# First mixer of a block kernel: its first two column blocks as one, pooling products placed inside other blocks, decay and forget rows spread by transfers, step sizes multiplied into x

## The chip, the cores and the metric

The kernel runs on one core of a Trainium2 chip. The metric is the device time of one execution in microseconds, as the median of several. Engines are named as the profile does: PE is TensorE, DVE is VectorE, ACT is ScalarE, POOL is GpSimd, SP is SyncE, whose queue issues the transfers.

## The reference, cut to what matters

A whole transformer block for 256 positions of width 2048 is followed by two more mixers (a forgetting attention and a retention layer). The change touches the first mixer and the attention:

```python
# first mixer: xbc, dt_raw, z, u are column ranges of hn @ w_in
xbc = silu(dwconv_centred(xbc, conv_w, conv_b)); xs, bm, cm = split(xbc)
dt = softplus(dt_raw + dt_bias)                  # two directions, 16 heads
acum = cumsum(dt * a); decay = exp(where(causal, acum[l] - acum[s], -inf))
y_diag = einsum("bclgn,bcsgn,bcgels,bcsgep->...", cm, bm, decay, xs * dt)
y = y_fwd + y_bwd + xs * d_skip; y = y * silu(z); y = y * rsqrt(mean(y*y)) * norm_w
y_pool = (windowed_mean(u) - u) @ pool_w[g] * pool_scale       # 4 groups of 256
mix = concat([y_ssd, y_pool]) @ w_out
# attention: c = cumsum(log_sigmoid(f_logit)), 16 heads of 128
s = q @ k.T * scale + c[q] - c[k];  s = where(key <= query, s, -inf);  softmax(s) @ v
```

## The kernel before, in words

All large products are f32 in quality, made from two fp32r halves. A piece of weights (mostly 128 x 1024, 512 KB) is loaded into one of four `raw` buffers; ScalarE copies it to `whi` (L1256), VectorE subtracts to get `wlo` (L1733); TensorE multiplies `whi` with both halves of the activations, side by side in 512 columns, and `wlo` with the high half in 256. A piece is a *use*. `layout()` (L99) makes the list of uses by hand, block after block, and `late(u, step)` puts each smaller step behind use u; every engine's program walks over the same list, so a step keeps its place on each engine's queue. In a program, steps placed with `late` for a use come ahead of the emptying of the block that ends with it (`place` with phase 1), except for those that the first loop of the vector program takes out (L1916: conv 0 and 2, z 0). Splits run five uses ahead (`AHEAD`), loads eight.

A column block of the first mixer ("turned") has 256 columns and all 16 k tiles: mostly four uses of four k tiles. It fills two tiles of PSUM, `bank[tile % 4]`; before its first product, TensorE waits (`emptied(n - 4)`) until VectorE has reduced the two halves of that bank into SBUF (`add_halves`, which the profile shows as TENSOR_REDUCE of line L1746). Two successive blocks thus use the two halves of the four main banks in turn; banks 4 to 7 serve small products.

Order of the first mixer: conv 8 (k tiles 0 to 3 in single uses, whose transfers also carry x, then three of four k tiles, with x loaded beside them), conv 10, conv 0, dt (32 columns), conv 2, 4, 6, pool 0 to 3, z 0, 2, 4, 6. A pooling product `pool_out` g (two k tiles, one use) is placed after pool 2, pool 3, z 0 and z 2. From the last use e of dt on, the heads follow:

- `cums` (e+6): cumulated decays, as columns (bank 6, `A`) and as 16 rows (bank 7), which ScalarE copies to `rowf` and `rows` (L1407, L1410) and VectorE completes in `rows[32:48]`.
- `decay` h: one product (L834, `bank<-rows,hot`) of 512 columns spreads row h over 128 partitions, from a one-hot column of `hot`.
- `decay_args` (L1425, four operations), `decay_exp` (L1431), `head_w` (four operations of VectorE that multiply with the step size `dtv` and with the products of C and B, `cbm`).
- `xnat` c: TensorE transposes two heads of x into bank 7 (L1102), ScalarE copies them out (L1414). `head_out` multiplies `xnat` with `W` and `wt` (8 f32 products for a pair of heads), and VectorE adds the result to S1.

In the attention, `scores` h ends with a product of `hot` and `rows` of 384 columns, which adds the forget row to both score tiles; `soft` adds the column and the mask.

Of the kernel before, what the change touches and what calls it, by code (L numbers as in the profile page):

```python
# [27 lines left out]
STARTS = [(0, 1), (1, 1), (2, 1), (3, 1), (4, 4), (8, 4), (12, 4)]  # L28
JOINED = 4
NEG = -1.0e30  # L30
# [68 lines left out]
def layout():  # L99
# [3 lines left out]
    def begin(kind, arg, operand, form="turned", cols=256):  # L103
        n = 2 if cols >= 256 else 1
        b = Block(kind, arg, operand, form, cols, count["tile"], n)
        count["tile"] += n
        return b
# [20 lines left out]
    def side_by_side(*blocks, form="turned", cols=256):  # L128
# [5 lines left out]
        return [u - 1, u]  # L134

# [90 lines left out]
    for i in range(4):  # L226
        late(i, "load_natural", i)
        late(i + 4, "x_squares", i)
    late(7, "x_factor")
    late(13, "hot")  # L230
# [6 lines left out]
    for c, col in ((8, 2048), (10, 2304), (0, 1024), (2, 1280), (4, 1536), (6, 1792)):  # L237
        e = block("conv", c, xa0, "w_in", col, STARTS if c == 8 else full)
        d, cuts = {8: 5, 10: 3}.get(c, 1), (0, 3, 5)
# [18 lines left out]
        if c < 8:  # L258
            for j in range(2):
                late(e + (8 if c == 0 else 6) + j, "xnat", c + j)  # L260
    for g in range(4):
        e = block("pool", g, xa0, "w_in", 2592 + 256 * g, full)
        late(e + 6, "pool_split", g)
        if g > 1:
            e = block("pool_out", g - 2, ("pin", g - 2), f"pool{g - 2}", 0, [(0, 2)])
            late(e + 1, "pool_out_split", g - 2)
    for c in (0, 2, 4, 6):
        e = block("z", c, xa0, "w_in", 128 * c, full)
# [8 lines left out]
        if c < 4:  # L277
            e = block("pool_out", 2 + c // 2, ("pin", 2 + c // 2), f"pool{2 + c // 2}", 0, [(0, 2)])
            late(e + 1, "pool_out_split", 2 + c // 2)
# [58 lines left out]
    for g in range(4):  # L338
# [20 lines left out]
        def heads(e, attend):  # L359
            for i, (n, late_by) in enumerate(zip((4, 5, 7, 8), attend)):  # L360
# [6 lines left out]
        if g < 3:  # L367
            values()
            if g == 0:
# [3 lines left out]
                late(e + 3, "forget_sums")  # L373
            gates(0)
# [114 lines left out]
def block_kernel(nc, a, out):  # L489
# [6 lines left out]
    with ExitStack() as ctx:  # L496
# [36 lines left out]
        hot = sb("hot", [128, 16], FR)  # L533
# [7 lines left out]
        x_in = {i: semaphore(f"x{i}") for i in range(JOINED, len(STARTS))}  # L541
        xn_in = [semaphore(f"xn{i}") for i in range(4)]
        pre_in, tables_in = semaphore("pre"), semaphore("tables")
        decay_in = [semaphore(f"decay{i}") for i in range(2)]
        par_in, con_in, counts_in, x_again, p_in, post_in, rows_in, stored = (
# [25 lines left out]
        W = [hflat[:, 1536 + 512 * i:1536 + 512 * i + 512] for i in range(2)]  # L571
        rcnt = hflat[:, 2560:3584]
        wt = [hflat[:, 3584 + 128 * i:3584 + 128 * i + 128] for i in range(4)]
# [3 lines left out]
        xnat = flat(S2[:, 0:8, :]).rearrange("p (s c) -> p s c", s=2)  # L577
# [3 lines left out]

        CONV = (8, 10, 0, 2, 4, 6)
# [27 lines left out]
        PT = [X[:, 768 + 384 * i:768 + 384 * i + 384] for i in range(2)]  # L610
        cn, fz, gains = sm[:, 0:32], sm[:, 32:64], sm[:, 519:520]
# [21 lines left out]
        HELD_BACK = (0, 1) + HELD + (MIX - 2, MIX - 1, MIX) + (GATE - 3, GATE - 2, GATE - 1, GATE, GATE + 1)  # L633
# [40 lines left out]
        tile_of = {(s.block.kind, s.block.arg): s.block.tile for s in uses}  # L674
        start_of = {s.block: u for u, s in reversed(list(enumerate(uses)))}
# [53 lines left out]
        def x_tile(j):  # L729
# [4 lines left out]
            return raw[i][:, T * (n + j - k0):T * (n + j - k0 + 1)]  # L734
# [6 lines left out]
        def sync_program(sp, q):  # L741
# [1929 lines left out]
```

## Time and profile before

| | us |
|---|---|
| median of 3 runs | 2367.84 (2367.78 to 2368.92) |
| profiled execution | 2367.74 |
| its span | 2366.0 |
| TensorE busy | 2351.8 (99%) |
| VectorE busy | 1622.6 (69%) |
| ScalarE busy | 1217.5 (51%) |
| GpSimd busy | 395.6 (17%) |
| chain that ended last | PE 95%, DVE 2%, ACT 1% |

Busy shares are averages over a long kernel; the first mixer is its first 217 us, the attention lies between about 1150 and 1600 us. Matmuls overlap in the pipeline, so the time that one costs is read from its start to the next one's start. A group of one form prints as one row with its count.

### The profile page before, as it was taken

The page shows a single profiled execution, that of the slowest core. Times are in us where ns is not written, and L with a number is a line of the kernel's source. Part 1 is how long each engine was busy: PE and PEld are TensorE (multiplying, and loading weights), DVE is VectorE, ACT ScalarE, POOL GpSimd, SP SyncE. Part 2 cuts the span into 40 slices and gives each one's busy share as a digit, 9 for nine tenths or more (in the row PEclk, how much of TensorE's full clock was granted, in tenths as well). Part 3 has the DMA queues.
Part 4 walks back from the last instruction along what each step waited for, and adds up shares of the span by engine and source line. Part 5 has one row for each costly group of instructions (what it writes and reads, how often), then busy time and mean ns, then how long its engine had stood idle before and what let it go on. Part 6 is the DMA issues. An engine that isn't in the chain of part 4 may idle for free.

```text
span 2366.0 us, 30059 instructions
## 1 busy us (share of the span) xinstructions
PE 2351.8 (99%) x11878; PEld 1981.0 (84%) x11878; DVE 1622.6 (69%) x2043; ACT 1217.5 (51%) x1647; POOL 395.6 (17%) x336
## 2 busy tenths in 40 slices
PE   9999999999999999999999999999999999999999
PEld 7878898888888888888788888887888888888887
DVE  7898578779877777775755556657666655666656
ACT  7866464445544444575655555535444444444442
POOL 1262016326424224300000000001000000000000
PEclk9999999999999999999999999999999999999999
DMA  8446655665666666665556465565665666656654
GB/s 297 156 146 197 213 178 185 199 190 172 213 203 191 188 191 205 202 200 176 180 180 211 153 198 165 164 188 166 193 182 182 221 185 195 180 179 189 187 179 125
DMA packets 122941, 444.05 MB, mean 188 GB/s; under 512 B 13744, under 2 KB 15408, under 8 KB 122288
## 3 DMA queue, kind: packets, MB, share of 16 engines
q1 hardware_dynamic: 122800, 442.12, 59.4%
q8 instruction: 94, 1.54, 0.3%
q14 instruction: 47, 0.39, 0.1%
HBM read 439.97 MB, written 2.10 MB: 187 GB/s over the span
## 4 chain that ended last, share of the span: by engine, by line
PE 95%; DVE 2%; ACT 1%; issue 0%; DMA 0%; SPq 0%; DVEq 0%; ACTq 0%
PE bank L834 94%; DVE wlo L1733 1%; ACT whi L1256 0%; PE bank L983 0%; DVE hT L1736 0%; DVE hn L1736 0%; PE bank L1242 0%; PE bank L1168 0%; ACT hT L1425 0%; PE bank L1190 0%; DMA hT<-in_xT 0%; DVE ev L1736 0%; ACT L1431 0%; DVE xa L1733 0%; DVE xa L1736 0%
## 5 line engine op out<-in xcount | busy, mean ns | idle before, releaser
L1733 DVE TENSOR_TENSOR wlo<-raw,whi 128x1024 fp32r<-128x1024 f32 (+2 forms) x811 | 1037.8, 1287 | 646.9 <-ACT whi L1256 644.6
L1256 ACT ACTIVATE whi<-raw 128x1024 fp32r<-128x1024 f32 (+2 forms) x813 | 847.0, 1048 | 873.2 <-PE bank L834 840.7
L834 PE MATMUL bank<-xa,whi 128*128 128x512 f32 (+1 forms) x2688 | 841.8, 395 | 5.6 <-DVE xa L1736 2.3
L834 PE MATMUL bank<-whi,xa 128*128 128x512 f32 x2048 | 636.1, 392 | 2.2 <-DVE wlo L1733 1.8
L834 PEld LDWEIGHTS bank<-xa,wlo 128*128 128x128 f32 x2656 | 497.7, 188 | 115.1
L834 PE MATMUL bank<-xa,wlo 128*128 128x256 f32 (+1 forms) x2656 | 521.1, 278 | 0.0
L834 PEld LDWEIGHTS bank<-whi,xa 128*128 128x128 f32 x2048 | 379.6, 188 | 79.6 <-DVE wlo L1733 2.4
L834 PE MATMUL bank<-whi,xb 128*128 128x512 f32 x1416 | 436.9, 390 | 0.0
L834 PEld LDWEIGHTS bank<-xa,whi 128*128 128x128 f32 x2688 | 411.3, 188 | 14.8 <-DVE wlo L1733 4.7
L834 PE MATMUL bank<-wlo,xa 128*128 128x512 f32 x1024 | 399.1, 390 | 0.0
L834 PEld LDWEIGHTS bank<-whi,xb 128*128 128x128 f32 x1416 | 264.8, 188 | 55.3 <-DVE wlo L1733 0.5
L834 PE MATMUL bank<-wlo,xb 128*128 128x512 f32 x708 | 275.7, 389 | 0.0
L834 PEld LDWEIGHTS bank<-wlo,xa 128*128 128x128 f32 x1024 | 192.2, 188 | 40.9
L2450 POOL TENSOR_TENSOR S<-S,rs 128x256 f32<-128x256 f32 x88 | 99.1, 1148 | 389.1 <-DVE S L1746 275.7
L834 PEld LDWEIGHTS bank<-wlo,xb 128*128 128x128 f32 x708 | 132.9, 188 | 27.7
L2450 POOL TENSOR_TENSOR ev<-ev,con 128x256 f32<-128x256 f32 x32 | 40.6, 1288 | 560.0 <-DVE ev L1746 560.0
L2450 POOL TENSOR_TENSOR hn<-hn,hT 128x512 f32<-128x512 f32 x4 | 7.9, 1974 | 626.2 <-DVE xa L1733 626.0
L834 PE MATMUL bank<-whi,xc 128*128 128x512 f32 x224 | 69.2, 390 | 0.0
L1746 DVE TENSOR_REDUCE S<-bank 128x256 f32<-128x512 f32 x88 | 56.5, 684 | 0.8 <-PE bank L834 0.6
L834 PEld LDWEIGHTS bank<-whi,xc 128*128 128x128 f32 x224 | 41.9, 188 | 8.8
L1746 DVE TENSOR_REDUCE ev<-bank 128x256 f32<-128x512 f32 (+1 forms) x66 | 42.6, 683 | 5.2 <-PE bank L834 5.2
L2450 POOL TENSOR_TENSOR S<-S 128x256 f32<-128x256 f32 x44 | 42.5, 985 | 11.0 <-ACT S L1574 11.0
(288 smaller groups left out, 1595.4 us busy)
## 6 DMA issues: line engine op xcount, KB each, us to landing
raw<-in_w SPq DMA_DIRECT2D x803, 512.0 KB, 3.7
hT<-in_ln_rows SPq DMA_DIRECT2D x2, 2048.0 KB, 8.8
raw<-in_w SPq DMA_DIRECT2D x9, 256.0 KB, 2.9
S<-in_x SPq DMA_DIRECT2D x4, 512.0 KB, 8.2
hT<-in_x SPq DMA_DIRECT2D x1, 2048.0 KB, 8.1
out<-S SPq DMA_DIRECT2D x8, 256.0 KB, 2.6
hT<-in_xT SPq DMA_DIRECT2D x3, 512.0 KB, 6.7
X<-in_post SPq DMA_DIRECT2D x2, 768.0 KB, 5.4
```

The source lines that it names most:

```text
L834: return pe.matmul(o, w, x, start=start, stop=stop, skip_group_check=True)
L1256: act.activation(hi, r, ACT.Copy).then_inc(*w_high(i))
L1733: return dve.tensor_tensor(o, x, y, op)
L1746: return dve.tensor_reduce(o, halves(b), AX, ALU.add)
L2450: return pool.tensor_tensor(o, x, y, op)
```

## The change

It has five parts.

1. `begin` lets a turned block have four tiles, and conv 8 and conv 10 become one block of 512 columns: four single k tiles, then six uses of two k tiles (`STARTS`). The x tiles 4 to 15 keep their three transfers (`X_LOADS`), now issued ahead of the weights at each step. `conv_add` empties all four tiles, ahead of the other work of its use. The natural loads and squares of x come one use later in number.
2. `around` puts a pooling product behind the first use of another block: `pool_out` 0 inside pool 3, `pool_out` 1 to 3 inside z 0, 2, 4.
3. `decay` and the one-hot product are gone. `store_sums` writes `rowf` to memory, `load_sums` h reads row h into all 128 partitions (four buffers in `hn`), and `decay_args` reads from there. All head steps come one use later.
4. `xnat` multiplies the transposed x with the step sizes of both directions on VectorE (`xdt`), in banks 7 and 5 alternately; `head_w` becomes one product of 768 columns.
5. In the attention, the one-hot product is gone; `load_forgets` reads the forget row into 128 partitions, GpSimd adds the mask (`mask_forgets`), and `soft` adds that row.

```diff
-STARTS = [(0, 1), (1, 1), (2, 1), (3, 1), (4, 4), (8, 4), (12, 4)]
+STARTS = [(0, 1), (1, 1), (2, 1), (3, 1)] + [(k, 2) for k in range(4, 16, 2)]
+X_LOADS = [(4, 4), (8, 4), (12, 4)]
...
+    def around(outer, inner):
+        b, c = (begin(*o[:3]) for o in (outer, inner))
+        for i, (k0, n) in enumerate(full):
+            u = use(b, *outer[3:], k0, n, first=i == 0, last=k0 + n == KT)
+            if i == 0:
+                v = use(c, *inner[3:], 0, 2)
+        return u, v
...
-        e = block("conv", c, xa0, "w_in", col, STARTS if c == 8 else full)
-        d, cuts = {8: 5, 10: 3}.get(c, 1), (0, 3, 5)
+        if c == 8:
+            e = block("conv", 8, xa0, "w_in", 2048, STARTS, cols=512)
+        elif c != 10:
+            e = block("conv", c, xa0, "w_in", col, full)
+        d, cuts = {8: 1, 10: 3}.get(c, 1), (0, 3, 5)
...
+            late(e + 7, "store_sums")
             for h in range(16):
-                t = e + (7 if h else 8) + 19 * (h // 2) // 4 + 2 * (h % 2)
-                late(t, "decay", h)
+                t = e + (8 if h else 9) + 19 * (h // 2) // 4 + 2 * (h % 2)
+                late(max(e + 8, t - 2), "load_sums", h)
                 late(t + 1, "decay_args", h)
...
     for g in range(4):
-        e = block("pool", g, xa0, "w_in", 2592 + 256 * g, full)
+        pool = "pool", g, xa0, "w_in", 2592 + 256 * g
+        if g == 3:
+            e, v = around(pool, pool_out(0))
+            late(v + 1, "pool_out_split", 0)
+        else:
+            e = block(*pool, full)
...
     for c in (0, 2, 4, 6):
-        e = block("z", c, xa0, "w_in", 128 * c, full)
+        z = "z", c, xa0, "w_in", 128 * c
+        if c < 6:
+            e, v = around(z, pool_out(1 + c // 2))
+            late(v + 1, "pool_out_split", 1 + c // 2)
+        else:
+            e = block(*z, full)
...
+            for i in range(4):
+                late(e, "load_forgets", 4 * g + i)
+                late(e + 3, "mask_forgets", 4 * g + i)
...
+                late(e + 5, "store_forgets")
...
-                        for i, (k0, n) in enumerate(STARTS):
+                        for i in range(4):
                             load(i)
-                            if i >= JOINED:
-                                sp.dma_start(hT[:, k0:k0 + n, :], x_view[:, k0:k0 + n, :]).then_inc(x_in[i], 16)
+                        for i, (k0, n) in enumerate(X_LOADS):
+                            sp.dma_start(hT[:, k0:k0 + n, :], x_view[:, k0:k0 + n, :]).then_inc(x_in[k0], 16)
+                            load(4 + i)
...
+                    elif step == "store_sums":
+                        q.wait_ge(*act_evac.of("rows"))
+                        sp.dma_start(row_sums[0], rowf).then_inc(sums_out, 16)
+                    elif step == "load_sums":
+                        h, = k
+                        q.wait_ge(sums_out, 16)
+                        if h >= 4:
+                            q.wait_ge(*act_evac.of("args", h - 4))
+                        sp.dma_start(decay_row[h % 4], row_sums[0][h:h + 1, :].broadcast_to((128, 2 * T))).then_inc(sums_in[h % 4], 16)
...
-                        q.wait_ge(*(act_evac.of("xnat", c - 1) if c else act_evac.of("rows")))
+                        if c > 1:
+                            q.wait_ge(*vec_val.of("xnat", c - 2))
+                        else:
+                            q.wait_ge(*(vec_val.of("cb", 1, 5) if c else act_evac.of("rows")))
                         q.wait_ge(*act_val.of("conv", c))
+                        B = bank[5 if c % 2 else 7]
...
-                    elif step == "decay":
-                        mm(B[:, :], hot[:, h:h + 1].broadcast_to((128, 128)), rows[:, :], True,
-                           True).then_inc(*side("decay", h))
...
-                                mm(bank[6][64 * i:64 * i + 64, 0:256], xnat[:, t, 64 * (h - 1 + i):64 * (h + i)],
-                                   W[i][:, 256 * t:256 * t + 256], t == 0)
+                                mm(bank[6][64 * i:64 * i + 64, 0:256], xdt[:, t, t, h - 1 + i, :],
+                                   W[i][:, 512 * t:512 * t + 256], t == 0)
...
-                        mm(B[:, 128:384], q_t[i][:, 128:256], k_t[i][:, :], False)
-                        mm(B[:, 0:384], hot[:, h:h + 1].broadcast_to((128, 128)), rows[:, 0:384], False,
-                           True).then_inc(*side("scores", h))
+                        mm(B[:, 128:384], q_t[i][:, 128:256], k_t[i][:, :], False, True).then_inc(*side("scores", h))
...
-                    if step == "conv" and k[0].arg in (0, 2):
+                    if step == "conv" and k[0].arg in (8, 0, 2):
                         conv_add(k[0])
...
-                        stt(w[:, 0:256], e_[:, 0:256], dtv[:, h:h + 1], c[:, 0:256], ALU.mult,
-                            ALU.mult).then_inc(*vec_val("w", h, 0))
+                        tt(W[h % 2], E[h % 2], cbm[h // 8], ALU.mult).then_inc(*vec_val.both(("w", h, 3), ("w", h, 5)))
+                    elif step == "xnat":
+                        c, = k
+                        B = bank[5 if c % 2 else 7]
+                        q.wait_ge(*vec_val.of("dtv"))
+                        q.wait_ge(sums_out, 16)
+                        q.wait_ge(*side.of("xnat", c))
+                        for s in range(2):
+                            x = B[:, 128 * s:128 * s + 128].rearrange("p (d h c) -> p d h c", d=1, h=2).broadcast_to((128, 2, 2, 64))
+                            f = dtv[:, 32 * s:32 * s + 32].rearrange("p (d h c) -> p d h c", d=2, c=1)[:, :, 2 * c:2 * c + 2, :]
+                            m = tt(xdt[:, s, :, 2 * c:2 * c + 2, :], x, f.broadcast_to((128, 2, 2, 64)), ALU.mult)
+                        m.then_inc(*vec_val("xnat", c))
...
+                    elif step == "mask_forgets":
+                        row, mask = forget_row[h % 4], cc("mask_qk")[:, 128:256]
+                        q.wait_ge(forgets_in[h % 4], 16 * (h // 4 + 1))
+                        tt(row[:, 0:128], row[:, 128:256], mask, ALU.add).then_inc(*pool_val("forgets", h, 0))
+                        tt(row[:, 256:384], row[:, 256:384], mask, ALU.add).then_inc(*pool_val("forgets", h, 1))
```

## Rows read from the trace of the kernel before

**Rows 1.** The page's part 1: busy time of each engine, whole span

```profile
PE 2351.8 (99%) x11878; PEld 1981.0 (84%) x11878; DVE 1622.6 (69%) x2043; ACT 1217.5 (51%) x1647; POOL 395.6 (17%) x336
```

**Rows 2.** Waits of TensorE, whole span: total, times, longest, in us

```profile
PE bank L834 <- DVE xa L1736: 2.3, 3, 1.4
PE bank L834 <- DVE ev L1746: 2.2, 2, 1.5
...
PE bank L1102 <- ACT S L1414: 1.1, 1, 1.1
PE bank L834 <- DVE X L1746: 0.9, 1, 0.9
```

**Rows 3.** Busy time by stretch: start:end, length, engines, clock, DMA share, GB/s

```profile
138.00:144.00 6.00, 6.00 (x43) 4.84 (x42) 6.00 (x7) 3.91 (x7) 5.14 (x6) 1.00 0.02 3
```

**Rows 4.** Timeline of TensorE, a decay product: start, length of the row

```profile
103.21 0.40 PE L834 MATMUL bank<-rows,hot 128*128 128x512 f32 x1
103.45 0.63 PE L834 MATMUL bank<-xa,whi 128*128 128x512 f32 x2
```

**Rows 5.** Timeline of TensorE in the attention: scores, then a turn

```profile
1228.47 0.52 PE L834 MATMUL bank<-rows,hot 128*128 128x384 f32 x1
1228.83 0.63 PE L834 MATMUL bank<-whi,xa 128*128 128x512 f32 x2
...
1256.48 0.70 PE L834 MATMUL bank<-xa,whi 128*128 128x512 f32 x2
1257.02 0.40 PE L834 MATMUL bank<-xa,wlo 128*128 128x256 f32 x2
```

**Rows 6.** Timeline of TensorE at the transposes of x (L1102)

```profile
84.87 0.40 PE L834 MATMUL bank<-rows,hot 128*128 128x512 f32 x1
86.41 0.44 PE L1102 MATMUL bank<-con,S 128*128 128x128 f32 x2 [1.14 <-ACT S L1414]
```

**Rows 7.** Timeline of ScalarE and TensorE at the start

```profile
4.13 0.42 ACT L1256 ACTIVATE whi<-raw 128x256 fp32r<-128x256 f32 x1 [1.90 <-DMA raw<-in_w]
...
5.61 1.19 PE L834 MATMUL bank<-xa,whi 128*128 128x512 f32 x2 [0.55 <-DVE xa L1736]
...
7.03 1.05 PE L834 MATMUL bank<-xa,whi 128*128 128x512 f32 x2
7.88 0.63 PE L834 MATMUL bank<-xa,wlo 128*128 128x256 f32 x2
...
15.43 0.70 PE L834 MATMUL bank<-xa,whi 128*128 128x512 f32 x2 [0.25 <-DVE xa L1736]
...
32.24 0.62 PE L834 MATMUL bank<-xa,whi 128*128 128x512 f32 x2
```

**Rows 8.** Timeline of TensorE at two ends of a pooling product

```profile
131.38 0.40 PE L834 MATMUL bank<-xc,wlo 128*128 128x256 f32 x2
131.89 1.00 PE L834 MATMUL bank<-xa,whi 128*128 128x512 f32 x2
132.73 0.40 PE L834 MATMUL bank<-xa,wlo 128*128 128x256 f32 x2
...
146.92 0.40 PE L834 MATMUL bank<-rows,hot 128*128 128x512 f32 x1
148.21 1.00 PE L834 MATMUL bank<-xa,whi 128*128 128x512 f32 x2 [0.89 <-DVE X L1746]
```

**Rows 9.** Timeline of VectorE around the second of them

```profile
141.16 3.45 DVE L1733 TENSOR_TENSOR wlo<-raw,whi 128x1024 fp32r<-128x1024 f32 x2
...
144.93 1.21 DVE L1733 TENSOR_TENSOR wlo<-raw,whi 128x1024 fp32r<-128x1024 f32 x1
146.06 1.40 DVE L1736 SCALAR_TENSOR_TENSOR hT<-hT,sm,S 128x256 f32<-128x256 f32 x4
147.38 1.28 DVE L1746 TENSOR_REDUCE X<-bank 128x256 f32<-128x512 f32 x2
```

**Rows 10.** The page's part 6: DMA issues, KB each, us to landing

```profile
out<-S SPq DMA_DIRECT2D x8, 256.0 KB, 2.6
```

More of the change, by code:

```diff
@@ L226, in layout @@
     for i in range(4):
[L227 to L230, printed above, removed]
+        late(i + 1, "load_natural", i)
+        late(i + 5, "x_squares", i)
+    late(8, "x_factor")
     late(11, "x_row")
@@ L532, in block_kernel @@
         sm = sb("sm", [128, 522])
-        hot = sb("hot", [128, 16], FR)
+        row_sums = [nc.dram_tensor(f"row_sums{i}", (16, n), F32, kind="Internal").ap() for i, n in enumerate((2 * T, T))]
         rows = sb("rows", [128, 2 * T], FR)
@@ L540, in block_kernel @@
         raw_in = [semaphore(f"raw{i}") for i in range(NRAW)]
-        x_in = {i: semaphore(f"x{i}") for i in range(JOINED, len(STARTS))}
+        x_in = {k0: semaphore(f"x{k0}") for k0, _ in X_LOADS}
         xn_in = [semaphore(f"xn{i}") for i in range(4)]
@@ L544, in block_kernel @@
         decay_in = [semaphore(f"decay{i}") for i in range(2)]
+        sums_out, sums_in = semaphore("sums_out"), [semaphore(f"sums{i}") for i in range(4)]
+        forgets_out, forgets_in = semaphore("forgets_out"), [semaphore(f"forgets{i}") for i in range(4)]
         par_in, con_in, counts_in, x_again, p_in, post_in, rows_in, stored = (
@@ L570, in block_kernel @@
         E = [hflat[:, 768 * i:768 * i + 768] for i in range(2)]
-        W = [hflat[:, 1536 + 512 * i:1536 + 512 * i + 512] for i in range(2)]
-        rcnt = hflat[:, 2560:3584]
-        wt = [hflat[:, 3584 + 128 * i:3584 + 128 * i + 128] for i in range(4)]
+        W = [hflat[:, 1536 + 768 * i:2304 + 768 * i] for i in range(2)]
+        rcnt = hflat[:, 3072:4096]
         cpad = [X[:, o:o + 260] for o in (6, 278, 550, 822)]
@@ L580, in block_kernel @@
         dtv, A, da = sm[:, 0:64], sm[:, 64:128], sm[:, 128:192]
+        decay_row = [hn[:, 1, 512 * i:512 * i + 512] for i in range(4)]
         CONV = (8, 10, 0, 2, 4, 6)
@@ L610, in block_kernel @@
         PT = [X[:, 768 + 384 * i:768 + 384 * i + 384] for i in range(2)]
+        forget_row = [flat(S2[:, 10:16, :])[:, 384 * i:384 * i + 384] for i in range(4)]
         cn, fz, gains = sm[:, 0:32], sm[:, 32:64], sm[:, 519:520]
@@ L674, in block_kernel @@
         tile_of = {(s.block.kind, s.block.arg): s.block.tile for s in uses}
+        tile_of["conv", 10] = tile_of["conv", 8] + 2
         start_of = {s.block: u for u, s in reversed(list(enumerate(uses)))}
@@ L1407, in scalar_program @@
                         act.activation(rowf, bank[7][0:16, :], ACT.Copy).then_inc(*act_evac("rows"))
-                        q.wait_ge(*act_evac.now())
-                        q.wait_ge(*act_val.of("no_rows"))
-                        act.activation(rows[0:16, :], rowf, ACT.Copy).then_inc(*act_val("rows"))
-                    elif step == "xnat":
-                        c, = k
-                        q.wait_ge(*side.of("xnat", c))
-                        act.activation(xnat[:, :, 128 * c:128 * c + 128],
-                                       bank[7][:, 0:256].rearrange("p (s t) -> p s t", s=2),
-                                       ACT.Copy).then_inc(*act_evac("xnat", c))
                     elif step == "decay_args":
                         h, = k
-                        q.wait_ge(*side.of("decay", h))
+                        q.wait_ge(sums_in[h % 4], 16 * (h // 4 + 1))
                         q.wait_ge(*vec_val.of("sums"))
@@ L1424, in scalar_program @@
                                                     (512, 768, 256, 48 + h)):
-                            m = act.activation(E[h % 2][:, first:last], bank[4 + h % 2][:, src:src + last - first],
+                            m = act.activation(E[h % 2][:, first:last], decay_row[h % 4][:, src:src + last - first],
                                                ACT.Relu, scale=-1.0, bias=A[:, n:n + 1])
@@ L1890, in conv_add @@
             def conv_add(b):
-                c = b.arg
-                for j in range(2):
-                    n = b.tile + j
+                for j in range(b.tiles):
+                    c, n = b.arg + j // 2 * 2, b.tile + j
+                    j = j % 2
                     q.wait_ge(*pool_val.of("pads"))
@@ L1944, in vector_program @@
                         dve.reciprocal(rsn[:, :], rsn[:, :]).then_inc(*vec_val("h_column", r))
-                    elif step == "conv" and k[0].arg not in (0, 2):
+                    elif step == "conv" and k[0].arg in (4, 6):
                         conv_add(k[0])
@@ L1978, in vector_program @@
                         dve.tensor_copy(A, bank[6][:, 0:64]).then_inc(*vec_val("sums"))
-                        q.wait_ge(*act_val.of("rows"))
-                        tt(rows[32:48, :], rowf, f32(rows[0:16, :]), ALU.subtract).then_inc(*vec_val("rows"))
                     elif step == "mask_cb":
```

83 lines of the change are left out of this document (31 added, 52 removed).

## The prediction, made before any run of the change

> **What bounds it now.** Four views, in this order. The page's busy times come first: TensorE is busy for 2351.8 of the 2366.0 us span [rows 1], which leaves 14.2 us idle. A change can therefore gain only by giving TensorE less to do, or by closing small gaps in it. TensorE's waits say where gaps are: 2.3 us on xa (the start), 2.2 us in two waits for ev and 0.9 for X (PSUM banks not yet emptied), 1.1 us in front of the transposes of x [rows 2]. The busy times by stretch name the next engine: in the first mixer VectorE works 6.00 of 6.00 us [rows 3], so whatever stands in its queue there delays what comes behind. The timelines give prices, taken from start to start, as the lengths of matmul rows overlap.
>
> The profiled execution took 2367.74 us (span 2366.0), 0.1 below the median of 2367.84; the sum is made against 2367.7. About 0.2% (4.7 us) is what a measurement of this kernel can tell from no change.
>
> **Term 1, decay products: -3.8.** The 16 products of a one-hot column with `rows` go. One starts at 103.21 and the next instruction at 103.45 [rows 4]: 0.24 us on TensorE, nothing beside it. 16 x 0.24 = 3.8.
>
> **Term 2, forget rows in the scores: -4.4.** The same product of 384 columns takes 0.36 us (1228.47 to 1228.83) [rows 5]. Not all of it returns. It is the step from f32 operands to fp32r ones, and whatever comes next now pays for that: a whi pair behind f32 transposes takes 0.54 (1256.48 to 1257.02) [rows 5], where two thirds of a full k tile's 0.70 (next terms) are 0.47. So 0.36 - 0.08 = 0.28, x16 = 4.4.
>
> **Term 3, transposes of x: -1.3.** At 84.87 TensorE stands until 86.41, 1.54 less the product's 0.24: ScalarE had to copy bank 7 before the next transpose [rows 6]. Afterwards two banks (5, 7) alternate, and VectorE empties them in the multiplication by the step size, with two pieces of slack. I count that one stall as gone and smaller ones as staying. The price is on VectorE: two operations of 2 x 128 columns in, 256 out per block, bounded by the reduction below (0.64) and by half of it each, so 0.6 to 1.3 us for each of 8 blocks; I take 0.75, 6 us. Against it, `head_w` becomes one operation of 768 columns, by three quarters of the split of 1024 (1.21) [rows 9] 0.91, where four took 1.40 [rows 9]: 16 x 0.49 = 7.8 less. VectorE comes out about even and nothing of it enters the sum; ScalarE loses its eight copies.
>
> **Term 4, the start: -0.4.** Before, the first eight k tiles run from 5.61 to 15.43, 9.8 us; the next 24 take 16.8 (to 32.24), 0.70 each [rows 7], so eight are worth 5.6 and 4.2 are lost. Of these, 1.75 are waits for x (2.3 less the 0.55 ahead of 5.61) [rows 2, 7]; the rest, 2.4, is TensorE at its lower rate: a whi pair takes 0.85 (7.03 to 7.88) [rows 7] instead of 0.47. The clock column of the windows does not show it; the durations do. With 512 columns under each k tile, TensorE has 1.4 us of work for each, more than x needs to arrive and be split, so the waits go: -1.75. The first piece is 384 KB instead of 256 and its split is twice as wide: the first product 0.8 later (0.4 for the bytes at the pace of the stretch, 0.2 on each of two engines). Of that 0.8, half comes back, as less work runs at the low rate. Together -1.4. But the double block fills all four banks of the main products, and the next block starts on the first at once: a reduction must empty it. At 147.38 such a pair begins and TensorE starts at 148.21 [rows 8, 9], 0.83 later; the second tile costs 0.38 more. The first tile ends 0.3 before the block does: about +1.0.
>
> **Term 5, moved pooling products: -0.1.** Now each short product lies between two blocks, and the block behind it needs banks that the block ahead has just filled. The four stalls: 0.28 (131.38 to 131.89, less 0.23) and 0.37 (the pair of 0.84) [rows 8]; 1.05 + 0.38 at 146.92; the two on ev, 2.2 idle [rows 2], with the 0.54 by which the third exceeds its shown 0.89 added to each, 3.3. Sum 5.4. After the change the short product sits inside the next block, so its own banks have a whole piece of slack; but the *outer* block's successor takes the outer block's banks with nothing in between. Two tiles per block and four banks: outer, inner, next puts next on outer's. Four such borders. Pool 3 to z 0: at this use the output of heads 6 and 7 is behind the last piece, and VectorE adds it to S1 (about 0.4) ahead of the reduction: 0.4 + 0.83 + 0.38, 1.6, say 1.7 with a handover. z 0 to z 2: this reduction is placed ahead of all else and lies under the products of heads 8 and 9: 0.2. z 2 to z 4 and z 4 to z 6: `head_w` is in front, 0.91, of which 0.4 fits before the block's end: 1.7 each. Sum 5.3, an exchange, not a removal. Bounds: 0.4 each where VectorE has caught up (1.6); 3 each with its lag of today (12).
>
> **Term 6, transfers through memory: 0.** Added on SP: one store and 16 loads of 256 KB for the decays, one store and 16 of 128 KB for the forgets. A store of 256 KB lands in 2.6 us [rows 10]; I take that for the tiny store too, and 3 for a load (no row shows a row spread over 128 partitions). Stored at use e+7, read at e+8, needed by ScalarE at e+10: 2.6 + 3 against three pieces of 2.8. Later loads are issued three uses ahead. SP stands for some 0.6 us at e+8 with weight loads behind it, which have four uses of slack. POOL adds the mask in 32 small operations, in a stretch where it has almost none. From below a load costs nothing, from above 1 us for each of 8 pairs of heads.
>
> Sum: -3.8 - 4.4 - 1.3 - 0.4 - 0.1 = -10.0, 2367.7 - 10.0 = **2357.7**, 2353.5 to 2361 by the bounds of terms 3 to 5 near their middle.
>
> **Two rules weighed.** Two splits of 1024 took 3.45 us at 141.16 where one takes 1.21 [rows 9], with POOL at 5.14 of 6.00 us busy [rows 3]: some 1.0 more through POOL. The Trainium skill, SBUF — State Buffer, section "SBUF: two separate sides", says the cause is an exclusive lock: a VectorE operation with two SBUF inputs waits for a whole GpSimd operation. By that rule the new `head_w` is exposed at each border and the sum would be that of rival B.
>
> The start is the other. The low rate ended while TensorE was in continuous work, and the change lengthens the pause ahead of it. The Trainium skill, TensorE: Matmul & The Clock Gate, section "Part 1: The HAM clock gate", holds that full rate is only released by sustained activity; by it the release could come later, rival C.
>
> **Rivals.**
> A, VectorE catches up at the borders (its products are fewer, and no decay product delays it): 0.9 instead of 1.7 at three borders, another 1.3 for smaller stalls: **2354**. Against it: 6.00 of 6.00 busy.
> B, POOL holds `head_w`: 1.0 more at three borders: **2360.7**.
> C, the clock rises later: half of 3 more us is lost, 1.5: **2359.2**.
> D, the change doesn't do its work: rows arrive late, and each pair of heads holds TensorE for 1 us: +8, **2365.7**. For it: no row has such a load; against: the slack of term 6.
> E, slower: VectorE falls one piece (2.8 us) behind its lag of 1.8 (pool 3 ends 1.4, two k tiles, ahead of 146.92, at 145.5; its reduction starts at 147.38 [rows 8, 9]). Then each of four borders costs 4.6 + 0.91 + 0.83 + 0.38 = 6.7, 26.9 instead of 5.3: 2357.7 + 21.6 = **2379.3**. It decides from 3.7 us more at each border. For it: VectorE is full, and the new operations on the transposes wait for TensorE at the head of its queue; against: its work is not more.
>
> **Chances.** Forecast 0.53, A 0.15, B 0.14, C 0.08, D 0.06, E 0.04. A, B and C are all faster than 2363.1: faster 0.90. D lies within 0.2%: 0.06. E: 0.04. The range 2352.5 to 2363 holds all but D, E and the tails.
>
> **What would show it.** No matmul from `rows` and `hot`; the scores' last product followed by a whi pair of 0.54; no wait at 85 on L1414; conv 0 starting 0.4 earlier than 32.24 with a stall just ahead of it; waits on the reduction at z 0, z 4 and z 6 of 1 to 2 us and nearly none at z 2; no ScalarE wait on the row transfers. Wrong if the borders sum to under 3 or over 9 us, if the first product comes after 7 us, or if TensorE waits behind head outputs.

## The result, and the profile after

The changed kernel takes 2372.01 us (17 runs, 2370.29 to 2375.82) where the kernel before takes 2367.93 beside it (17 runs): ratio 1.0016, interval [1.0009, 1.0022]. It is 4.1 us slower. The forecast was 10.0 faster, with a range of 2352.5 to 2363.0, so it was wrong in sign, though the difference lies within the 0.2% that the prediction called no change. The profiled execution took 2371.46 us.

The page's part 1 after, beside [rows 1]:

```profile
PE 2347.2 (99%) x11846; PEld 1977.5 (83%) x11846; DVE 1621.4 (68%) x2007; ACT 1215.3 (51%) x1630; POOL 423.4 (18%) x368
```

TensorE is busy for 4.6 us less, as a removal of work should show, and the span is 3.6 longer (2369.6): its idle time rose from 14.2 to 22.4 us, and part of its busy time was spent at half rate. The waits of TensorE, whole span (total, times, longest), answer to [rows 2]:

```profile
PE bank L882 <- DVE X L1767: 6.9, 2, 4.1
PE bank L882 <- DVE xa L1757: 3.5, 3, 1.8
PE bank L882 <- DVE ev L1767: 3.0, 2, 2.1
...
PE bank L1154 <- ACT S L1436: 0.2, 1, 0.2
```

The wait for the copy of bank 7 has gone (1.1 to 0.2). X, a bank that no reduction has emptied yet, holds TensorE 6.9 us instead of 0.9, one wait being 4.1. The waits on xa, the start, grew instead of vanishing. The head outputs are waited for (`hT`, 1.2 us in two waits), which they were not before.

Where the time stands is read by setting the same product of both timelines side by side (after less before, us):

| TensorE reaches | before | after | difference | in this stretch | predicted |
|---|---|---|---|---|---|
| the dt block | 43.83 | 51.81 | +8.0 | +8.0 | -0.4 |
| the mixer's output | 207.47 | 213.58 | +6.1 | -1.9 | -5.2 |
| the last attention product | 1533.90 | 1537.33 | +3.4 | -2.7 | -4.4 |
| its end (span) | 2366.0 | 2369.6 | +3.6 | +0.2 | 0 |

The first line rests on these two rows, the one before the change and the one after:

```profile
43.83 4.31 PE L834 MATMUL bank<-xa,whi 128*64 128x512 f32 x18
```

```profile
51.81 4.31 PE L882 MATMUL bank<-xa,whi 128*64 128x512 f32 x18
```

Of the 14.3 us between forecast and result (medians; 4.1 of them are the loss itself), 8.4 arise before 52 us. TensorE at the end of the double block:

```profile
32.71 0.64 PE L882 MATMUL bank<-xa,wlo 128*128 128x256 f32 x4
37.44 1.30 PE L882 MATMUL bank<-xa,whi 128*128 128x512 f32 x2 [4.09 <-DVE X L1767]
...
38.96 1.05 PE L882 MATMUL bank<-xa,whi 128*128 128x512 f32 x2
39.81 0.63 PE L882 MATMUL bank<-xa,wlo 128*128 128x256 f32 x2
```

VectorE, which must empty the four banks, in the same stretch, and ScalarE ahead of it:

```profile
31.25 1.23 DVE L1754 TENSOR_TENSOR wlo<-raw,whi 128x1024 fp32r<-128x1024 f32 x1 [1.95 <-ACT whi L1297]
34.76 1.23 DVE L1754 TENSOR_TENSOR wlo<-raw,whi 128x1024 fp32r<-128x1024 f32 x1 [2.29 <-ACT whi L1297]
35.99 0.16 DVE L1957 TENSOR_REDUCE rsn<-sm 128x2 f32<-128x8 f32 x1
36.51 0.17 DVE L1959 RECIPROCAL rsn<-rsn 128x2 f32<-128x2 f32 x1 [0.36 <-ACT rsn L1410]
36.60 2.48 DVE L1767 TENSOR_REDUCE X<-bank 128x256 f32<-128x512 f32 x4
```

```profile
33.67 1.06 ACT L1297 ACTIVATE whi<-raw 128x1024 fp32r<-128x1024 f32 x1 [1.23 <-DMA raw<-in_w]
```

The block's last products end near 33.2. VectorE is idle from 32.5 to 34.76, 1.6 us of it with the banks full, and yet does not reduce: at the head of its queue stands the split of the last piece of conv 0 (use 13), which TensorE needs only three pieces after the restart, at 49.0. That split waits for ScalarE's copy, and the copy for a transfer that lands at 33.67. Then follow x_factor's two small steps, and at 36.60 the reduction. TensorE resumes 4.3 us late. And it resumes slowly: a whi pair takes 0.85 (38.96 to 39.81) instead of 0.47 until 42.8. Busy times by stretch (start:end, length, PE, PEld, DVE, ACT, POOL, granted clock, DMA share, GB/s):

```profile
4.30:33.00 28.70, 25.17 (x129) 21.04 (x129) 19.68 (x29) 21.74 (x41) 0.00 (x0) 0.94 0.99 371
33.00:37.40 4.40, 0.35 (x3) 0.14 (x2) 2.27 (x5) 3.41 (x8) 0.00 (x0) 0.89 0.98 369
37.40:43.00 5.60, 5.57 (x17) 4.67 (x18) 3.42 (x5) 0.85 (x1) 0.00 (x0) 0.50 0.64 210
```

TensorE was busy for 0.35 of 4.40 us, and in the next stretch its granted clock is 0.50, the 1.2 GHz level, until 42.8. The DMA column fits a late piece: the queues are full (0.99, 371 GB/s) from the first transfer to the restart. It does not prove the cause, as they were as full before the change (0.99, 379 GB/s in the same 28.7 us).

### The profile page after: what moved, and what is told of

The parts are those of the page before. It is cut to its first block, busy times and chain, and to the rows that moved or that the text cites. A ratio compares the mean times of both kernels' runs of the same rounds, so it can differ in the third digit from the quotient of the medians.

```text
span 2369.6 us, 30012 instructions
## 1 busy us (share of the span) xinstructions
PE 2347.2 (99%) x11846; PEld 1977.5 (83%) x11846; DVE 1621.4 (68%) x2007; ACT 1215.3 (51%) x1630; POOL 423.4 (18%) x368
## 4 chain that ended last, share of the span: by engine, by line
PE 92%; DVE 4%; ACT 1%; DMA 1%; issue 0%; SPq 0%; DVEq 0%; ACTq 0%
PE bank L882 91%; DVE wlo L1754 2%; DMA raw<-in_w 1%; DVE ev L1757 1%; ACT whi L1297 0%; PE bank L1031 0%; DVE hT L1754 0%; DVE hn L1757 0%; DVE X L1767 0%; PE bank L1283 0%; PE bank L1212 0%; PE bank L1231 0%; DVE xa L1757 0%; DMA row_sums<-S 0%; ACT hT L1450 0%
## 5 line engine op out<-in xcount | busy, mean ns | idle before, releaser
L1754 DVE TENSOR_TENSOR wlo<-raw,whi 128x1024 fp32r<-128x1024 f32 (+1 forms) x810 | 1045.2, 1298 | 652.5 <-ACT whi L1297 650.8
L2467 POOL TENSOR_TENSOR S<-S,con 128x128 f32<-128x128 f32 x32 | 21.1, 694 | 457.8 <-DMA S<-row_sums 457.8
```

The source lines that it names most:

```text
L1754: return dve.tensor_tensor(o, x, y, op)
L2467: return pool.tensor_tensor(o, x, y, op)
```

## The experiments

Twelve kernels ran, in three groups, each beside the kernel before (medians 2367.92, 2367.94 and 2368.72 us). Theory one: the start and the pooling borders gave back what the other parts won, since reductions stand in VectorE's queue behind splits that wait for transfers, and the stall lets the clock fall. The rivals: the loss is in the transfers for rows or the new operations on x; x_factor alone holds the reduction; or the stall is harmless, and the clock alone costs.

**start_as_before** takes the double block back and leaves the rest:

```diff
-STARTS = [(0, 1), (1, 1), (2, 1), (3, 1)] + [(k, 2) for k in range(4, 16, 2)]
+STARTS = [(0, 1), (1, 1), (2, 1), (3, 1), (4, 4), (8, 4), (12, 4)]
...
-            e = block("conv", 8, xa0, "w_in", 2048, STARTS, cols=512)
+        e = block("conv", c, xa0, "w_in", col, STARTS if c == 8 else full)
```

> The changed kernel with part 1 undone: conv 8 and conv 10 as two blocks, natural loads, squares and factor of x at their old uses, x transfers in their old order. Theory: of the 4.1 us by which the changed kernel is slower, the start costs 8.0 (dt begins at 51.81 instead of 43.83), and the rest gains 3.9; so this kernel runs in 2364, 4 under the kernel before, dt near 43.8, and the clock of 37 to 43 us stays at 1.00. Rival: the loss of the start is made up later by slack (VectorE catches up while TensorE stands), then less than 8 comes back and the time is 2367 or more.

Measured 2363.88, ratio 0.9982 [0.9974, 0.9991]; dt begins at 44.44. **start_alone** puts the double block into the kernel before, by the same lines turned round.

> The kernel before with part 1 of the change alone. Theory: plus 8.0, 2376, with one stall of some 4.7 us at the border to conv 0 and the low clock behind it. Rival (the loss comes from part 1 together with the later x_factor and other parts): under 2372.

Measured 2376.23, 1.0036 [1.0023, 1.0048]: 8.3 us slower than before. TensorE waits there as in the change:

```profile
32.66 0.63 PE L841 MATMUL bank<-xa,wlo 128*128 128x256 f32 x4
38.68 1.30 PE L841 MATMUL bank<-xa,whi 128*128 128x512 f32 x2 [5.38 <-DVE X L1753]
```

The start costs 8.1 us within the change (2372.0 - 2363.9) and 8.3 alone: it adds up within the noise, and without it the rest of the change gains 4.0. That rules out the transfers for rows and the operations on x as the place of the loss.

**factor_later** moves x_factor behind the reduction.

```diff
-    late(8, "x_factor")
+    late(10, "x_factor")
```

> The changed kernel with x_factor at use 10 instead of 8, so that VectorE reduces the four banks of the double block before it waits for the squares of x. Theory one: the sum and the reciprocal (35.99 to 36.60) are only the last part of what is ahead; the split of the piece that lands late (34.76 to 35.99) stays in front of the reduction, so the stall shrinks by 0.6 and the time by 0.6, 2371.4. Theory two: the wait for the squares is what holds VectorE: the stall falls to 1 us and the clock does not drop, 2365.

Measured 2372.25, 1.0018 [1.0009, 1.0027]: nothing. VectorE:

```profile
35.51 1.23 DVE L1754 TENSOR_TENSOR wlo<-raw,whi 128x1024 fp32r<-128x1024 f32 x1 [2.31 <-ACT whi L1297]
36.65 2.48 DVE L1767 TENSOR_REDUCE X<-bank 128x256 f32<-128x512 f32 x4
```

The reduction starts at 36.65 all the same. Counted from the start of the split it comes 0.7 us sooner (1.14, where the change takes 1.84), so x_factor did hold it for that long; but the split itself starts 0.75 later in this execution, behind a copy that starts at 34.42 instead of 33.67. It is the late split that decides. The double block ended 1.4 earlier here (31.8), and TensorE restarted at 37.48, as in the change: while the reduction waits for a transfer, nothing that makes TensorE's block shorter is of use.

**reduce_first** keeps x_factor late and puts the split of use 8 behind the reduction.

```diff
-                if 0 <= u < N - AHEAD and u not in HELD_BACK:
+                if 0 <= u < N - AHEAD and u not in HELD_BACK and u != 8:
+                    if u == 9:
+                        split(8 + AHEAD)
```

> The changed kernel in which VectorE reduces the four banks of the double block ahead of the split of the late piece (use 8's split placed behind the reduction of use 9, x_factor at 10). Factor_later showed the reduction beginning at 36.65 right behind the split of 35.51. Theory: that split, which waits for a transfer, is what holds the reduction: now it begins at about 33 and TensorE stands for some 1.0 us instead of 4.3 to 5.7, the clock stays at 1.00, x_row comes at about 39.5 instead of 45.80, and the time falls by 6, to 2366. Rival: TensorE then waits for the late pieces themselves (ScalarE's copy of that piece begins only at 33.7): a stall of the same size moves a few us later, 2370 or more.

Measured 2367.46, 0.9998 [0.9989, 1.0007], 4.5 us less than the change. VectorE and TensorE:

```profile
32.13 1.22 DVE L1754 TENSOR_TENSOR wlo<-raw,whi 128x1024 fp32r<-128x1024 f32 x1 [2.96 <-ACT whi L1297]
33.27 2.48 DVE L1767 TENSOR_REDUCE X<-bank 128x256 f32<-128x512 f32 x4
```

```profile
30.91 0.64 PE L882 MATMUL bank<-xa,wlo 128*128 128x256 f32 x4
34.10 1.00 PE L882 MATMUL bank<-xa,whi 128*128 128x512 f32 x2 [2.55 <-DVE X L1767]
...
41.03 0.71 PE L882 MATMUL bank<-con,rsn 128*128 128x128 f32 x4 [0.81 <-DVE rsn L1961]
```

The order of the queue is the cause, shown: the reduction comes 3.3 earlier, the stall is 2.7, the clock stays at 1.00 there, and dt begins at 47.17 instead of 51.81. But what holds the reduction now is the split ahead of it, which waited 2.96 for its own copy, and the row of x's factors (con, rsn) is late next.

**reduce_first_2** puts the splits of uses 7 and 8 behind it (`u not in (7, 8)`, both splits at use 9).

> Reduce_first left a stall of 3.1 us, as the split of the piece before (32.13 to 33.27, it too waited for its transfer) still stood ahead of the reduction. Here that one is placed behind it as well. Theory: the reduction begins as the block ends, near 31, the stall at the border is 0.8 + 0.4, 1.9 less than in reduce_first; but x_row waits for the squares of x, which come no earlier, so most of the gain is met there (it waited 1.0 us in reduce_first, now up to 2.9): 2366.5 to 2367.5. Rival: the split itself is what TensorE needs next, and the stall only moves to the use after: 2367.5 with a stall on wlo.

Measured 2368.15, 1.0000 [0.9992, 1.0009]. The border is nearly gone, and the time is not:

```profile
31.93 1.00 PE L882 MATMUL bank<-xa,whi 128*128 128x512 f32 x2 [0.59 <-DVE X L1767]
...
41.28 1.12 PE L882 MATMUL bank<-con,rsn 128*128 128x128 f32 x4 [3.22 <-DVE rsn L1962]
```

TensorE reaches x_row at 41.28, against 41.03 with the border stalled: the wait has moved on, to the factors of x, whose reciprocal now stands at 41.06 behind a split that waits. Before the change x_row ran at 35.02. Behind this wait of 3.2 the clock falls again (granted clock 0.66 in 40 to 45 us), and dt begins at 48.99. In both orders dt is still later than before the change (43.83): no order tried here makes the double block worth having.

**tables_later** issues the loads of par and con two and six uses later, so that pieces of weights go first.

```diff
-    late(4, "load_par")
+    late(6, "load_par")
...
-    late(6, "load_con")
+    late(12, "load_con")
```

> The changed kernel with the loads of par and of the first columns of con (337 KB) behind the weights of use 14 instead of use 12, and the tables (640 KB) at use 12 instead of 6. If the late pieces are late because 400 GB/s of transfers are all in use, the piece whose split stands ahead of the reduction lands 0.9 us earlier: the copy at 33.67 comes at 32.8, the reduction at 35.7 instead of 36.60, the time 2371.1 or less, and the later pieces no longer wait. If they are late because they are issued late (25.1, when a raw buffer comes free), nothing moves.

Measured 2371.37, 1.0012 [1.0003, 1.0021]. ScalarE's copy begins at 33.35, not 32.8 as expected, and the reduction at 36.27 (36.60 in the change). The direction agrees with a chain of transfers and its size is a third of what I expected. The interval overlaps that of the change, so this is the trace's word alone, and why the piece lands late stays open: a transfer that is issued late is a rival that this run does not exclude.

**keep_busy** has TensorE multiply zeros into an unused bank while it waits, and **keep_busy_short** does so 9 times instead of 16.

```diff
+                if u == 9:
+                    for _ in range(16):
+                        mm(bank[7][:, 0:T], rs[:, 0:128], rs[:, :], True, True)
```

> The changed kernel with 16 products of zeros into the idle bank 7 behind the last piece of the double block (some 3.6 us of work in a stall of 4.7). If the idle stretch is what lets the clock fall, the clock of 37 to 43 us stays at 1.00, a whi pair there takes 0.47 instead of 0.85, and the time falls by 2.4, to 2369.6, at an unchanged stall. If the low clock has another cause, it stays and the time is 2372.

> Keep_busy again with 9 products instead of 16, as 16 took 6.7 us and pushed the next block from 37.44 to 39.50; there the clock stayed at 1.00, and from that start to x_row took 5.8 us instead of 8.4. With 9 (3.8 us, ending near 36.9) the next block starts at 37.4 as in the changed kernel. If idleness alone lets the clock fall, it stays up: x_row near 43.2 and 2.6 us less than the changed kernel, 2369.4. If the stretch needs to be filled to its end, the clock falls and the time is 2372.

Measured 2372.61, 1.0018 [1.0009, 1.0027], and 2371.26, 1.0014 [1.0005, 1.0022]. The stretches of the long one:

```profile
33.00:37.40 4.40, 4.40 (x22) 3.88 (x21) 2.36 (x5) 3.52 (x8) 0.00 (x0) 1.00 1.00 363
37.40:43.00 5.60, 5.60 (x31) 4.87 (x30) 3.33 (x5) 0.75 (x1) 0.00 (x0) 1.00 0.64 219
```

In the short one TensorE is busy for 4.11 of the 4.40 us and 5.38 of the 5.60, also at 1.00. With TensorE kept at work, the granted clock stays at 1.00, the 2.4 GHz level, and from the restart to x_row it takes 5.8 us in the long one (39.50 to 45.26) and 6.0 in the short one (37.58 to 43.54), where the change takes 8.4 (37.44 to 45.80). So the fall costs about 2.5 us. The sixteen products took 6.7 us, longer than the stall, and gave that back. In the short one x_row came 2.3 earlier; 1.5 of it is left at the end of the profiled execution, and 0.8 in the median, less than these intervals can tell from nothing. A second fall followed there at a pooling border (granted clock 0.66 in 151 to 156 us).

That second fall comes and goes, and it blurs the comparisons of these runs by up to some 1.3 us. TensorE stands 2.8 us in front of z 0 in the change and restarts at full rate; it stands as long in start_as_before and restarts at the low one:

```profile
153.41 1.01 PE L882 MATMUL bank<-xa,whi 128*128 128x512 f32 x2 [2.79 <-DVE X L1767]
```

```profile
145.04 1.13 PE L877 MATMUL bank<-xa,whi 128*128 128x512 f32 x2 [2.78 <-DVE X L1762]
...
146.40 1.05 PE L877 MATMUL bank<-xa,whi 128*128 128x512 f32 x2
147.25 0.63 PE L877 MATMUL bank<-xa,wlo 128*128 128x256 f32 x2
```

From the restart to the pooling product inside z 0 the first takes 3.17 us and the second 4.73. The profiled executions of factor_later, reduce_first, reduce_first_2, tables_later and keep_busy_short fall there too (keep_busy does not), for 1.1 to 2.2 us. Some 0.8 to 0.9 comes back, as TensorE then waits only 1.2 to 1.4 in front of z 4 instead of 2.1. Why the same wait lets the clock fall in one execution and not in another stays open.

**borders_early** keeps the start as before and puts the reductions of pool 3 and of z ahead of all else in their use.

```diff
-                    elif step == "z" and k[0].arg == 0:
+                    elif step == "z":
                         z_add(k[0])
+                    elif step == "pool" and k[0].arg == 3:
+                        pool_add(k[0])
```

> The changed kernel with the start as before (start_as_before, 2363.9) and the reductions of pool 3 and of all z blocks placed first in VectorE's queue at their use. In start_as_before the borders into z 0, z 4 and z 6 cost 3.4, 1.7 and 1.4 us, and the clock fell behind the first. Theory: the order on VectorE (split, then S1 or head_w, then reduction) makes two thirds of that: z 0 falls to about 1.0, z 4 and z 6 to 1.2 each, 3 us less and 1.6 more where the clock stays up: 2360. Rival: VectorE is late by work of earlier uses, the order within a use matters little: 2363.5.

**pooling_as_before** keeps the start as before and puts the pooling products back between the blocks.

```diff
-        if g == 3:
-            e, v = around(pool, pool_out(0))
...
+        e = block(*pool, full)
+        late(e + 6, "pool_split", g)
+        if g > 1:
+            e = block(*pool_out(g - 2), [(0, 2)])
```

> The changed kernel with the start as before and the pooling products back in their old places (part 4 of my account, moved pooling products, undone as well). The prediction held the move for an exchange (5.3 against 5.4 us). By the traces its borders cost 6.5 to 7.4 us against 5.4, so this kernel should be 1 to 3 us faster than start_as_before: 2362. If the placement inside a block is worth something, it is slower: 2365.

Measured 2361.2, 0.9971 [0.9959, 0.9982], and 2361.5, 0.9974 [0.9964, 0.9984], both against 2363.88 with the moved products in the change's queue order. By the medians, moving the pooling products costs 2.4 us, and placing the reductions first wins 2.7. The three intervals overlap, and of the three profiled executions only that with 2363.88 has the fall of the clock behind z 0, so the direction is backed by the waits below and the sizes are rough. TensorE's waits for reductions in the one and in the other:

```profile
PE bank L877 <- DVE ev L1762: 2.3, 3, 0.8
...
PE bank L877 <- DVE X L1762: 0.7, 1, 0.7
```

```profile
PE bank L875 <- DVE ev L1760: 2.3, 1, 2.3
...
PE bank L875 <- DVE X L1760: 1.0, 1, 1.0
```

Moved, there are four short waits; not moved, two, of which one is long. From row to row, with 0.38 for the second tile of each, the two unmoved ones come to about 4.4 us, where the kernel before had 5.4 in five: the other parts of the change had shortened them already, which the prediction's exchange of 5.3 for 5.4 left out.

**before_best** takes both: start and pooling products as before, reductions first. What is left of the change are the rows by transfers, the step sizes on x and the merged head_w.

> Start as before, pooling products in their old places, and the reductions of pool 3 and of the z blocks first in VectorE's queue: parts 3, 4 and 5 of the change alone, with the order on VectorE mended. In pooling_as_before two borders still cost 1.5 and 2.8 us (VectorE has 1.4 us of cover there, but head_w and a split in front); in borders_early the order took 2.7 us off. Both together: those 4.4 us fall to under 1, and the time to 2358, 10 under the kernel before, which is what the prediction expected of the change as a whole. Rival: VectorE is behind by more than the order inside a use can mend: 2361.

Measured 2358.49, 0.9956 [0.9944, 0.9969], 10.2 us faster than before; the waits for ev and X are gone from its list, and no stretch behind 10 us shows a granted clock under 1.00. It beats both kernels. That this is about the 10.0 of the forecast is luck: the forecast took 4.4 us for the forget rows, which give 2.9, and had no term for reductions placed first, which this kernel has instead of parts 1 and 2.

**forgets_alone** puts only the forget rows by transfer into the kernel before.

```diff
-                        mm(B[:, 128:384], q_t[i][:, 128:256], k_t[i][:, :], False)
-                        mm(B[:, 0:384], hot[:, h:h + 1].broadcast_to((128, 128)), rows[:, 0:384], False,
-                           True).then_inc(*side("scores", h))
+                        mm(B[:, 128:384], q_t[i][:, 128:256], k_t[i][:, :], False, True).then_inc(*side("scores", h))
```

> The kernel before with part 5 alone: the forget rows through memory, the mask added on GpSimd, no one-hot product in the scores. The prediction priced it at 4.4 us, from 0.36 less 0.08 for each head. In the changed trace the stretch from forget_turn to the last attend product shrank by 2.8, since the whi pair behind the scores takes 0.65, not 0.54. So 2365.1; with the predicted price 2363.5.

Measured 2365.80, 0.9986 [0.9977, 0.9995] against 2368.72: -2.9, with an interval of -5.4 to -1.2. Its trace and that of the change agree on the reason: the whi pair behind the scores takes 0.65 us in both (here 1230.30 to 1230.95; the rows of the change stand under Term 2 below).

## Why the prediction was wrong

**Term 4, the start (-0.4, measured +8.0), is the step that failed**, in three places. By the prediction the double block would end 1.4 earlier than the two blocks of before, near 30.8; it ended at 33.2. "TensorE has 1.4 us of work for each, more than x needs to arrive and be split" did not hold for the fifth k tile, the first of x's own transfers. It started at 12.15 before and at 14.74 in the change, so behind the first product the waits for x are 2.3 us (3.5 less the 1.18 ahead of 6.24), 1.75 before:

```profile
12.15 0.70 PE L834 MATMUL bank<-xa,whi 128*128 128x512 f32 x2 [1.44 <-DVE xa L1736]
```

```profile
14.74 1.16 PE L882 MATMUL bank<-xa,whi 128*128 128x512 f32 x4 [1.81 <-DVE xa L1757]
...
16.41 1.91 PE L882 MATMUL bank<-xa,whi 128*128 128x512 f32 x4
18.12 1.05 PE L882 MATMUL bank<-xa,wlo 128*128 128x256 f32 x4
```

In factor_later, reduce_first, reduce_first_2 and tables_later it starts between 14.05 and 14.92, with waits of 0 to 2.1 us behind the first product: x arrives when it does. In 5 to 33 us the queues are full in both kernels (0.99; 10.6 MB before, 10.4 after), and the change puts wider pieces of weights ahead of x (384 KB for 256); that the bytes set the pace is likely by these figures, and no run tested it. Twelve k tiles of 1.40 from 14.74 end near 31.7, which makes 0.9 of the 2.4. The other 1.5 is the clock, which fell here too: a whi group of four takes 1.71 (16.41 to 18.12) instead of 0.93. That part cost nothing in the end, as factor_later shows, which ended the block at 31.8 and restarted at the same time.

Next, the border was priced at 1.0 ("a reduction must empty it", with 0.83 for it) from a border at which VectorE had work in hand [rows 9]. That a reduction is ready as soon as the products end holds only if nothing ahead of it waits. Here a split for a piece needed later did, and the stall was 4.3 us. The prediction asked what the reduction takes and not what stands in front of it, though it did ask that at the pooling borders. The Trainium skill, PSUM — Partial Sum Buffer, section "Engine vs sequencer instructions", says that VectorE's queue is strictly first in, first out; by that rule a late piece stops the reduction as well, and this trace agrees, with VectorE idle until 34.76 in front of a reduction whose banks had been full since 33.2.

Last, the fall of the clock behind the border, 2.5 us, stood in no term. Rival C had a low rate at the first products. In the change those ran at full rate (a whi group of four 0.99, 6.24 to 7.23), and the low rate came at 16.4 and again behind the stall; in factor_later, reduce_first_2 and tables_later the first products did run at the low rate (6.36, a group of four in 2.05), and the fifth k tile started no later for it (14.05 to 14.92). The Trainium skill, TensorE: Matmul & The Clock Gate, section "Part 1: The HAM clock gate", says that idle time brings the throttle back; the granted clock of 0.50 behind the stall and of 1.00 with filler products agrees, while the full rate behind the 2.8 us at 153.41 shows that not every wait does it. So 2.4 (the block's end, 33.2 for 30.8) + 3.5 (4.3 of stall, and 0.2 at the second tile, for 1.0) + 2.5 make 8.4, the whole of what Term 4 missed.

**Term 1, decay products (-3.8)** cannot be measured apart here, but no product from rows is left, and the stretch from dt to the mixer's output can be added up: -3.8, -1.8 for the transposes (stalls of 1.30, 0.30 and 0.24 before, at 84.87, 81.26 and 99.68), +2.0 for the borders, +2.4 for new waits ahead of the head outputs (0.70 and 0.84), at 100.8 (0.38) and in front of the sums (0.45). That is -1.2 for the -1.9 measured; 0.7 stays unexplained.

**Term 3, transposes (-1.3)** was right where it looked: 1.1 became 0.2. It counted nothing for what comes next. The head outputs, with no decay product before them, now catch up with VectorE; the sign of being wrong "if TensorE waits behind head outputs" was met, in front of them:

```profile
104.25 0.39 PE L882 MATMUL bank<-xa,wlo 128*128 128x256 f32 x2
105.17 1.52 PE L882 MATMUL bank<-hT,S 128*64 128x256 f32 x16 [0.53 <-DVE hT L1754]
```

**Term 2, forget rows (-4.4, measured -2.7 in the change and -2.9 alone)** had the mechanism and not the size. The product's 0.36 went. The step that it hid was taken from a whi pair behind 128-column transposes, 0.08; behind the scores themselves the pair takes 0.65, 0.18 more than 0.47:

```profile
1234.23 0.82 PE L882 MATMUL bank<-S 128*128 128x128 f32 x4
1234.69 0.81 PE L882 MATMUL bank<-whi,xa 128*128 128x512 f32 x2
1235.34 0.40 PE L882 MATMUL bank<-wlo,xa 128*128 128x512 f32 x1
```

0.36 - 0.18 = 0.18, x16 = 2.9. The row that the prediction used was one step too far from the place.

**Term 5, pooling products (-0.1, measured +2.0)**: the borders sum to 7.4 instead of 5.3 (5.4 before). Each is the gap plus 0.38 for the second tile. z 0 to z 2 cost nothing, as said, and z 4 to z 6 1.4 for 1.7. Pool 3 to z 0 cost 3.3 for 1.7, and z 2 to z 4 2.7 for 1.7:

```profile
181.96 0.40 PE L882 MATMUL bank<-xa,wlo 128*128 128x256 f32 x2
184.46 1.00 PE L882 MATMUL bank<-xa,whi 128*128 128x512 f32 x2 [2.11 <-DVE ev L1767]
```

```profile
148.96 3.31 DVE L1754 TENSOR_TENSOR wlo<-raw,whi 128x1024 fp32r<-128x1024 f32 x2
152.19 0.47 DVE L1757 SCALAR_TENSOR_TENSOR S<-S,par,bank 128x256 f32<-128x256 f32 x1
152.58 1.28 DVE L1767 TENSOR_REDUCE X<-bank 128x256 f32<-128x512 f32 x2
...
181.62 1.23 DVE L1754 TENSOR_TENSOR wlo<-raw,whi 128x1024 fp32r<-128x1024 f32 x1 [0.66 <-ACT whi L1297]
182.76 0.95 DVE L1754 TENSOR_TENSOR hT<-hT,S 128x768 f32<-128x768 f32 x1
183.63 1.28 DVE L1767 TENSOR_REDUCE ev<-bank 128x256 f32<-128x512 f32 x2
```

The list ahead of the reduction was right (the output's addition, head_w), but the splits in front of both belonged to it, and VectorE came to them late: the reduction begins 3.6 us behind pool 3's last product (149.0) and 1.4 behind that of z 2 (182.2). That is the lag of rival E, at about half its price (3.3 and 2.7 for 6.7). Rival B had head_w held by POOL. By the exclusive lock of the Trainium skill, SBUF — State Buffer, section "SBUF: two separate sides", that could be; head_w took 0.95 at 182.76 against the 0.91 taken, so at this border the lock cost nothing, but POOL was idle there (from 177.6 to 184.40). With POOL at work, head_w took 1.50 in the change (145.99), and the two splits at 148.96 took 3.31 where two of 1.21 at a step of 1.13 [rows 9] take 2.3: some 1.0 of the first border. That agrees with the lock and does not prove it; no run took POOL's work away.

**Term 6, transfers (0)** was right for TensorE, with both sizes off. The page's part 6 shows the loads at 4.3 us for 3 taken, and the tiny store (32 KB) took 4.4 for 2.6. SP stood 1.6 for 0.6, in front of weight loads that had slack, and ScalarE waited once, 2.2 us at 90.89, for the first row:

```profile
hn<-row_sums SPq DMA_DIRECT2D x16, 256.0 KB, 4.3
```

The chances were the other fault. The only rival on the slower side needed VectorE a whole piece behind at four borders. None asked what a late transfer does at the one border that the change made new, where the transfers were busy without a gap.

## What to carry to other kernels

A block that fills all PSUM banks makes its successor wait for whatever stands ahead of the reduction in the emptying engine's queue. Read that queue back to its transfers and put the reduction ahead of splits that are needed later; where that queue waits for a transfer, a shorter block of TensorE only lengthens the wait. And price a removed instruction by what its neighbour takes at that very place, not at a similar one.

## What the runs showed that I had not expected

- A stretch with TensorE busy 0.35 of 4.40 us was followed by one at the 1.2 GHz level, worth 2.5 us, more than half of the stall itself. The stall of 2.7 us in reduce_first was followed by none, and the one of 2.8 in front of z 0 by one in six profiled executions and by none in two.
- In 15 to 20 us, with TensorE busy 5.00 of 5.00, the granted clock was 0.66 in the change, and 1.00 in factor_later, in which that part of the program is the same. In the 5 us before, TensorE was busy for 3.19 in the change, with the wait of 1.81 at its end, and for 4.13 in factor_later, with one of 0.87. In reduce_first such a wait of 1.50 was followed by 1.00. The medians of the change and of factor_later do not differ.
- A whi pair of fp32r products takes 0.18 us more behind f32 products of 256 columns, and 0.08 more behind f32 transposes of 128.
